# Retention heads: three rounded passes for most products, remainders on GpSimd, rings of two buffers, states updated in place

## The reference, cut to what matters

```
scores = einsum('bihd,bjhd->bhij', qc, kc) * decay_mask
intra  = einsum('bhij,bjhe->bihe', scores, vc)
cross  = einsum('bihd,bhde->bihe', qc * q_dec, S)
S_new  = S * chunk_dec + einsum('bjhd,bjhe->bhde', kc * k_dec, vc)
out    = intra + cross
```

## Time and profile before

| | us |
|---|---|
| median of 3 runs | 1812.44 (1810.49 to 1814.74) |
| the profiled execution | 1811.87 |
| its span | 1810.2 |
| TensorE busy in the span | 1758.1 |
| VectorE busy | 969.4 |
| ScalarE busy | 778.2 |
| GpSimd busy | 267.0 |

### The profile page before, as it was taken

One profiled execution on the slowest core, in us unless ns is written; L12 is line 12 of the kernel. 1 busy time (PEld: TensorE's weight loads), 2 busy tenths in 40 slices (PEclk: granted clock), 3 DMA queues, 4 the chain that ended last, 5 costly groups with the idle time before them and its releaser, 6 DMA issues. The chain is left out here.

```text
span 1810.2 us, 27358 instructions
## 1 busy us (share of the span) xinstructions
PE 1758.1 (97%) x9783; PEld 1388.7 (77%) x9783; DVE 969.4 (54%) x1867; ACT 778.2 (43%) x1683; POOL 267.0 (15%) x324
## 2 busy tenths in 40 slices
PE   5999999999999999999999999999998998999998
PEld 2678787878787878777788877788887777677677
DVE  4653535454444444453645554676625667777762
ACT  3742323232323232331434433353326768888720
POOL 2000000000000000000000011101113545555300
PEclk9999999999999999999999999999999999999999
DMA  9231312122222222366433578423365449696252
GB/s 338 87 97 60 95 61 89 67 79 76 75 80 68 87 61 93 104 209 217 130 84 116 190 231 271 157 80 112 102 186 134 123 117 251 194 236 190 86 192 93
DMA packets 153898, 240.60 MB, mean 133 GB/s; under 512 B 13289, under 2 KB 102177, under 8 KB 152770
## 3 DMA queue, kind: packets, MB, share of 16 engines
q1 hardware_dynamic: 136778, 179.69, 33.5%
q0 software_dynamic: 17024, 59.66, 9.3%
HBM read 177.91 MB, written 61.42 MB: 132 GB/s over the span
## 5 line engine op out<-in xcount | busy, mean ns | idle before, releaser
L488 PE MATMUL rt_acc<-rt_w_hi,rt_h_hi 128*128 128x512 f32 x504 | 203.3, 403 | 1.0 <-DVE rt_h_lo L1030 1.0
L490 PE MATMUL rt_acc<-rt_w_hi,rt_h_lo 128*128 128x512 f32 x504 | 197.1, 391 | 0.0
L489 PE MATMUL rt_acc<-rt_w_lo,rt_h_hi 128*128 128x512 f32 x504 | 196.5, 390 | 0.0
L1722 POOL TENSOR_TENSOR pa_take<-pa_take,pa_after_key 128x512 f32<-128x512 f32 (+2 forms) x152 | 153.3, 1011 | 141.7 <-DVE pa_after_key L2044 137.8
L1073 DVE TENSOR_TENSOR rt_by_cos<-rt_raw,rt_cos 128x256 f32<-128x256 f32 (+1 forms) x72 | 30.5, 424 | 243.9 <-ACT rt_raw L903 243.9
L914 ACT COPY rt_qk_t<-rt_tr 128x256 f32<-128x256 f32 (+1 forms) x72 | 26.0, 361 | 278.4 <-PE rt_tr L722 278.4
L2992 PE MATMUL kq_acc<-kq_w_hi,kq_h 128*128 128x512 f32 x320 | 128.6, 402 | 0.0
L2995 PE MATMUL kq_acc<-kq_w_hi,kq_h 128*128 128x512 f32 x320 | 125.1, 391 | 0.0
L2993 PE MATMUL kq_acc<-kq_w_lo,kq_h 128*128 128x512 f32 x320 | 124.7, 390 | 0.0
L1932 ACT ACTIVATE pa_keep<-z,pa_bias 128x128 f32<-128x128 f32 (+3 forms) x192 | 111.1, 600 | 5.9 <-PE z L1786 5.7
L1932 ACT ACTIVATE pa_take<-z,pa_bias 128x128 f32<-128x128 f32 (+3 forms) x192 | 111.1, 603 | 0.0
(11 more groups left out here) (406 smaller groups left out, 4025.8 us busy)
## 6 DMA issues: line engine op xcount, KB each, us to landing
ro_a_raw<-retained SPq DMA_DIRECT2D x14, 1024.0 KB, 6.0
rt_w_raw<-in_ret_w_in SPq DMA_DIRECT2D x16, 512.0 KB, 5.2
rt_w_raw<-in_ret_w_in SPq DMA_DIRECT2D x8, 1024.0 KB, 7.8
rt_old<-in_state_ret SPq DMA_DIRECT2D x8, 1024.0 KB, 5.9
rt_g_raw<-in_ret_w_in SPq DMA_DIRECT2D x8, 1024.0 KB, 5.2
out_st_sample<-rt_new POOLq DMA_DIRECT2D x8, 1024.0 KB, 7.9
k_cols<-kq_parts POOLq DMA_DIRECT2D x16, 512.0 KB, 4.0
kq_w_raw<-in_sb_w_in SPq DMA_DIRECT2D x4, 2048.0 KB, 10.2
```

The source lines that it names most:

```text
L488: nc.tensor.matmul(dst, h_hi[:, k, cols], w_hi[:, k, :], start=k == 0, stop=False)
L489: nc.tensor.matmul(dst, h_hi[:, k, cols], w_lo[:, k, :], start=False, stop=False)
L490: last = nc.tensor.matmul(dst, h_lo[:, k, cols], w_hi[:, k, :], start=False, stop=k == KD - 1)
L1722: nc.gpsimd.tensor_tensor(own, own, later, ALU.mult).then_inc(weighed, 1)
```

## The change

In heads 1 to 7, tiles 0 to 6, `attend` does its 20 products (two for tile 0, three for the others) in three rounded passes. The hi parts are made where the values are made: v_hi and q_hi by an added copy on ScalarE, k_hi, probs_hi and state_hi by an added instruction on VectorE. The remainders are made on GpSimd in a fixed order, and all count up one semaphore `rests`; `attend(t)` waits for the count `rests_by(h, t)` before its first matmul. v_lo lies over v and probs_lo over probs.

R becomes 2, and `probs` has one buffer. The samples' new states are written over `old`; `new` is gone. All stores move from GpSimd's queue to SyncE's, where the next `old` is loaded after the store of the one before. The waits `state_free`, `new_free` and `o_free` become waits for the stores themselves.

```diff
-        R = 3
+        R = 2
...
+        PARTED = NPT - 1
+
+        def parted(opens, t):
+
+            return not opens and t < PARTED
+
+        PER_HEAD = 5 * PARTED - 2
+
+        def rests_by(h, t):
+
+            kv, q, st, pr = 2 * min(t + 2, PARTED), min(t + 1, PARTED - 1), t, t + 1
+            return (h - 1) * PER_HEAD + (kv + q + st + pr)
...
+            def store_states(h):
+                sp.wait_ge(state_ready, after(h, NPT - 1))
+                sp.dma_start(t_out["st_prompt"][0, 0][bass.ds(h, 1)].rearrange("o k e -> (o k) e"), state[:]).then_inc(state_stored, 16)
+                sp.wait_ge(new_ready, h + (CR + 1))
+                sp.dma_start(t_out["st_sample"][0].rearrange("b h k e -> h k b e")[bass.ds(h, 1)].rearrange(
+                    "o k b e -> (o k) b e"), old[:]).then_inc(old_stored, 16)
+
+            def store_kept(h, cols):
+                kept = ps.retained[bass.ds(h * DV, DV), :].rearrange("(u p) c -> p u c", p=P)
+                sp.dma_start(kept[:, :, cols], o_t[:, :, cols]).then_inc(o_stored, 16)
+
+            load_old(0)
+            load_gates_of(0)
+            load_ada(0)
+            with sp.Fori(0, H - 1) as h:
+
+                sp.wait_ge(projected, h * NT + (NT + CR))
+                w_of.load(sp, t_in, h + 1)
+                store_states(h)
+                load_ada(h + 1)
+                sp.wait_ge(old_stored, h * 16 + 16)
+                load_old(h + 1)
+                load_gates_of(h + 1)
+                sp.wait_ge(o_out, h * TURNS + 4)
+                store_kept(h, slice(SEQ, SEQ + NS))
+                sp.wait_ge(o_out, h * TURNS + (TURNS + 1))
+                sp.sem_inc(storing, 1)
+                store_kept(h, slice(0, SEQ))
...
+            store_states(H - 1)
+            sp.wait_ge(o_stored, (H - 1) * 32)
...
+            def rest_of_state(h, t):
+                pool.wait_ge(state_ready, after(h, t))
+                nc.gpsimd.tensor_tensor(state_lo[:], state[:], state_hi[:].bitcast(F32), ALU.subtract).then_inc(rests, 1)
+
+            def rest_of_probs(h, t):
+                pool.wait_ge(masked, after(h, t))
+                nc.gpsimd.tensor_tensor(probs_lo[:], probs[:], probs_hi[:].bitcast(F32), ALU.subtract).then_inc(rests, 1)
+
+            def rest_of_q(h, t):
+                pool.wait_ge(turned_out, after(h, t))
+                nc.gpsimd.tensor_tensor(q_lo[:, t % R, :], qk_t[:, t % R, 0, :], q_hi[:, t % R, :].bitcast(F32),
+                                        ALU.subtract).then_inc(rests, 1)
+
+            def rest_of_v(h, t):
+                pool.wait_ge(taken, after(h, t))
+                nc.gpsimd.tensor_tensor(v_lo[:, t % R, :], v[:, t % R, :], v_hi[:, t % R, :].bitcast(F32), ALU.subtract).then_inc(rests, 1)
+
+            def rest_of_k(h, t):
+                pool.wait_ge(rotated, after(h, t))
+                nc.gpsimd.tensor_tensor(k_lo[:, t % R, :], rot[:, t % R, 1, :], k_hi[:, t % R, :].bitcast(F32),
+                                        ALU.subtract).then_inc(rests, 1)
+
+            with pool.Fori(1, H) as h:
+                for t in range(PARTED + 2):
+                    if 0 < t - 1 < PARTED:
+                        rest_of_q(h, t - 1)
+                    if 0 <= t - 3 < PARTED - 1:
+                        rest_of_state(h, t - 3)
+                    if 0 <= t - 2 < PARTED:
+                        rest_of_probs(h, t - 2)
+                    if t < PARTED:
+                        rest_of_v(h, t)
+                        rest_of_k(h, t)
...
+            def attend(h, t, opens):
+
+                r, slot, into = rows(t), t % R, out[0:rows(t), 0, 0:DV]
                 pe.wait_ge(o_taken, freed(h, t, 1))
                 if t == NPT:
+                    pe.wait_ge(masked, after(h, t))
                     pe.wait_ge(old_loaded, (h + 1) * 16)
                     pe.wait_ge(k_own_s, h + 1)
                     for i in range(2):
...
                             b, tokens = 4 * (c % 2) + 2 * (c // 2) + i, slice(32 * (c % 2), 32 * (c % 2) + 32)
                             nc.tensor.matmul(out[32 * c:32 * (c + 1), 0, 0:DV], q_diag[:, b, tokens], old[:, b, :], start=i == 0,
                                              stop=i == 1 and c >= 2, tile_position=(0, 32 * c))
-                elif t > 0:
-                    pe.wait_ge(state_ready, after(h, t - 1))
-                    nc.tensor.matmul(out[0:r, 0, 0:DV], qk_t[:, t % R, 0, :], state[:], start=True, stop=False)
-                last = nc.tensor.matmul(out[0:r, 0, 0:DV], probs[0:r, t % R, 0:r], v[0:r, t % R, :], start=t == 0, stop=True)
-                if t < NPT:
+                    nc.tensor.matmul(into, probs[0:r, 0:r], v[0:r, slot, :], start=False, stop=True)
+                elif parted(opens, t):
+                    pe.wait_ge(rests, rests_by(h, t))
+                    nc.tensor.matmul(into, probs_hi[:], v_hi[:, slot, :], start=True, stop=False)
+                    nc.tensor.matmul(into, probs_hi[:], v_lo[:, slot, :], start=False, stop=False)
+                    nc.tensor.matmul(into, probs_lo[:], v_hi[:, slot, :], start=False, stop=t == 0)
+                    if t:
+                        nc.tensor.matmul(into, q_hi[:, slot, :], state_hi[:], start=False, stop=False)
+                        nc.tensor.matmul(into, q_hi[:, slot, :], state_lo[:], start=False, stop=False)
+                        nc.tensor.matmul(into, q_lo[:, slot, :], state_hi[:], start=False, stop=True)
                     pe.wait_ge(state_ready, freed(h, t, 1) if t else h * NT + CR)
-                    last = nc.tensor.matmul(st[:, 0, 0:DV], rot[0:r, t % R, 1, :], v[0:r, t % R, :], start=True, stop=True)
+                    nc.tensor.matmul(st[:, 0, 0:DV], k_hi[:, slot, :], v_hi[:, slot, :], start=True, stop=False)
+                    nc.tensor.matmul(st[:, 0, 0:DV], k_hi[:, slot, :], v_lo[:, slot, :], start=False, stop=False)
+                    last = nc.tensor.matmul(st[:, 0, 0:DV], k_lo[:, slot, :], v_hi[:, slot, :], start=False, stop=True)
                 else:
+                    pe.wait_ge(masked, after(h, t))
+                    pe.wait_ge(state_ready, after(h, t - 1) if t else h * NT + CR)
+                    if t:
+                        nc.tensor.matmul(into, qk_t[:, slot, 0, :], state[:], start=True, stop=False)
+                    nc.tensor.matmul(into, probs[:], v[:, slot, :], start=t == 0, stop=True)
+                    last = nc.tensor.matmul(st[:, 0, 0:DV], rot[:, slot, 1, :], v[:, slot, :], start=True, stop=True)
+                if t == NPT:
...
+                if parted(opens, t):
+                    last.then_inc(raw_taken, 1)
+                    last = nc.scalar.copy(v_hi[:, t % R, :], src[:, 2 * DK:QKV])
                 last.then_inc(taken, 1)
...
-                nc.scalar.copy(qk_t[:, t % R, :, 0:r], src).then_inc(turned_out, 1)
+                last = nc.scalar.copy(qk_t[:, t % R, :, 0:r], src)
+                if t and parted(opens, t):
+                    last = nc.scalar.copy(q_hi[:, t % R, :], tr[:, 0, 0:P])
+                last.then_inc(turned_out, 1)
...
+                    dve.wait_ge(raw_taken, (h - 1) * PARTED + (t + 1))
...
+                    last = nc.vector.tensor_tensor(k_hi[:, t % R, :], by_cos[:, 1], by_sin[:, 1], ALU.add)
+                last.then_inc(rotated, 1)
...
+                dve.wait_ge(attended, freed(h, t, 1))
+                last = nc.vector.tensor_tensor(probs[0:r, 0:r], sc[0:r, 0, 0:r], table, ALU.mult)
+                if parted(opens, t):
+                    last = nc.vector.tensor_tensor(probs_hi[:], sc[:, 0, 0:P], table, ALU.mult)
+                last.then_inc(masked, 1)
...
-                    dve.wait_ge(state_free, h + 1)
+                    if not opens:
+                        dve.wait_ge(state_stored, h * 16)
+                    if parted(opens, t + 1):
+                        nc.vector.tensor_scalar(state_hi[:], st[:, 0, 0:DV], decay, None, ALU.mult)
                     nc.vector.tensor_scalar(state[:], st[:, 0, 0:DV], decay, None, ALU.mult).then_inc(state_ready, 1)
                 elif t < NPT:
                     dve.wait_ge(state_ready, after(h, t - 1))
                     nc.vector.tensor_tensor(state_sum[:], st[:, 0, 0:DV], state[:], ALU.add).then_inc(own, own_n.up())
                     dve.wait_ge(own, own_n.now())
+                    if parted(opens, t + 1):
+                        nc.vector.tensor_scalar(state_hi[:], state_sum[:], decay, None, ALU.mult)
                     nc.vector.tensor_scalar(state[:], state_sum[:], decay, None, ALU.mult).then_inc(state_ready, 1)
                 else:
                     join(h)
-                    dve.wait_ge(new_free, h + 1)
                     for n, src in enumerate((acc[:, 0], acc[:, 1], st[:, 0], tr[:, 0])):
                         pair = slice(2 * n, 2 * n + 2)
-                        last = nc.vector.tensor_tensor(new[:, pair, :], src.rearrange("p (b e) -> p b e", b=2),
```

(71 more changed lines are left out.)

51 lines of the change are left out of this document (21 added, 30 removed).

## The result

The changed kernel takes 1938.35 us (median of 4 runs, 1937.44 to 1939.40) against 1811.49 (4 runs, 1810.49 to 1814.74) for the kernel before in the same comparison. The ratio is 1.0695, 95% interval 1.0678 to 1.0712: 7% slower, 127 us. The forecast was 1905 with a range from 1868 to 1955, so the time is in the range and 33 us above its centre.

A forecast was written before the change was run, and what follows sets the result against it. TensorE, busy for 97% of the span, was taken to bound the kernel. Three passes -9.8, stalls +100.4, first head +1.5 and end +1 sum to +93 on 1811.87: 1905 us, range 1868 to 1955.

The forecast's parts named there:

- Gain of three passes: In seven heads, 20 products each take three rounded passes, 0.36 us in place of 0.43: 9.8 us gained.
- The queue order as the cause: attend(t) waits for probs_lo behind the next tile's q_lo on GpSimd: 14.3 us a head, 100.4 us lost in all.
- GpSimd's 128 columns: A remainder of 128 columns on GpSimd was priced at 0.41 us, from its rate on float32 products.
- the hand-over to TensorE: From a GpSimd result to TensorE's next start, 0.15 us was taken, between 0.05 and 0.3.
- attend(6), 0.76: At each head's attend(6), after the short sample tile, TensorE stalls 0.76 us because its own inputs come late.
- Head 0: In the first, float32 head, rings of two delay take and the input's splitting, before products 4 and 6: 1.5 us lost.
- The end: At the kernel's end the 1 MB state store stands ahead of two loads: 1 us lost, at worst 3.5.
- rival (c): TensorE's clock falls under repeated pauses, for half of each projection in 42 stalled tiles: 115 us more, 2020 us; chance 5%.
- both signs: Earlier clock readings: 0.67 with TensorE busy 6.41 of 10 us, but 1.00 with it busy 2.67 of 5.
- Rival (a): The remainders are hidden from TensorE, so the change gives its 9.8 us: 1802 us; chance 4%.
- (b): GpSimd is slow at the subtraction because writing the rounded type doubles its time: 1969 us, 1944 to 1980; chance 12%.
- (d): GpSimd's instructions overlap and short ones take less, so the middle five stalls are about 1 us: 1835 to 1870; chance 8%.

The follow-up runs named there:

- e2: The changed kernel with q's remainder moved behind those of state and probs in GpSimd's queue, and q counted one tile less in attend's wait: 1816.00 us.
- e5: e2 with rings of three for raw, rot, v and the hi and lo parts of k and v: 1805.42 us, ratio 0.9958 to the kernel before.
- e3: The changed kernel with a semaphore of its own for q's remainder, GpSimd's queue order left as it was: 1940.33 us.
- e7: The changed kernel with the remainder of probs computed twice on GpSimd, once into a tile nobody reads: 1967.01 us.
- e1: The changed kernel with eight unread 512-column matmuls on TensorE ahead of six of the seven waits in a head: 1914.96 us.
- e4: The changed kernel with all products in float32 and no GpSimd remainders, keeping rings of two, states in place and stores on SyncE: 1816.81 us.
- e6: The changed kernel with q's remainder between those of state and probs in GpSimd's queue: 1888.36 us.
- e8_g_later: e5 with VectorE's two remainders of the g weights moved behind rotate in their tiles: 1805.33 us.

## Why the prediction was right, and where its size was off

- **Gain of three passes, 9.8 us: right.** Steps of 0.12 after the first, and tiles of 7.00 in place of 7.21 wherever nothing waits (e2, e5).
- **The queue order as the cause, 100.4 us: right.** Forecast per head 1.73, five of 2.37 and 0.76; found 1.73 for attend(0), 2.41, and mostly 0.38 for attend(6), which makes 99 us. GpSimd's 128 columns took 0.45 and not 0.41, its 256 columns 0.72 and not 0.64, while the hand-over to TensorE was 0.06 (292.58 to 292.64) and not 0.15; these cancel. e2 shows the order as the cause, e3 clears the common semaphore, and e7 shows that each GpSimd instruction counts in full.
- **attend(6), 0.76: found 0.38 and, at the full clock in e1, 0.89.** The lower clock hides part of it.
- **Head 0, 1.5 us: right.** Before, TensorE waited once for h_lo in this head. It now waits three times, and the two new waits are 0.80 and 0.82 us, together 1.6, in TensorE's timeline:

```profile
79.61 0.50 PE L488 MATMUL rt_acc<-rt_w_hi,rt_h_hi 128*128 128x512 f32 x1 [0.80 <-DVE rt_h_lo L1106]
...
95.21 0.50 PE L488 MATMUL rt_acc<-rt_w_hi,rt_h_hi 128*128 128x512 f32 x1 [0.82 <-DVE rt_h_lo L1106]
```

- **The end, 1 us: found none.** ScalarE takes up the loaded block of the earlier trace rows at 904.36, 4 us before TensorE's product of that block, which starts at 908.37 with no wait, as before. The state store takes 4.4 us to land on SyncE's queue where it took 7.9 on GpSimd's. Row of the DMA issues:

```profile
out_st_sample<-rt_old SPq DMA_DIRECT2D x8, 1024.0 KB, 4.4
```

- **Left out: the first step after a pause.** It is 0.22 where the others are 0.12: 0.1 x 49 = 5 us.
- **The step that was off: the clock was left out of the sum.** I took it as rival (c) alone, at 115 us and 5%, priced as half of each projection in all 42 stalled tiles. In fact three tiles a head run at the lower level for some 3.4 us each (72 us in 21 tiles) and take 11.03 in place of 9.50. That is 1.53 x 21 = 32 us. In attend(6) it hides 0.5 x 7 = 3.5 of them, which the 99 above already leave out, so 28 to 29 remain to be gained; e1 gives 27 in the seven heads and 23 by the medians. So the mechanism of (c) was there at a quarter of its price, on top of the forecast and not in its place. The earlier trace rows held both signs, and I should have put a middle value into the sum instead of an all-or-nothing rival.

The account: -9.8 + 99 + 5 + 1.6 + 32 = 128 us, against 127 measured. e1's sum at the full clock is -9.8 + 103 + 5 + 1.6 = 100 us, and at the last head's sample tile its trace is 99.9 us behind the kernel before (853.73 against 753.88); the medians give 102.5. Less the clock and the first steps the measured 127 are 90, against a forecast of 93: the rest of the sum held, partly by errors that cancel. That the time lies in the stated range is in part luck: the range reached up to 1955 to allow for a slower GpSimd and slower hand-overs, and what filled it was mostly the clock.

Rival (a), remainders hidden, is what e2 and e5 make true: the 9.8 us came out as 6.7 in e5. Rivals (b) and (d) fall by the 0.45 and 0.72 us that the remainders took, one after the other without overlap.

What stays open: why the clock falls in every second tile and not in each, and why e4's median is 4 us above the kernel before when only some 2.5 are placed. For the first, e3 is a warning: its pauses and tiles are a little longer (2.33 in 9.57), and yet the lower level stands for less, 61 us in 18 stretches, and not in every second tile.

## What to carry to other kernels

When work moves to an idle engine, write down for each item when its input comes and when its output is due, and check the order of the queue against both. Here an item due a whole tile later stood ahead of the two that were due at once, which cost 122 of 127 us in a change that was to save TensorE time. Price repeated short pauses of TensorE twice, once as time and once as the chance of the lower clock behind them. And when a ring is shortened, look at the shortest tile, not the typical one: there the wait came first.

## What the runs showed of the hardware

- **The clock.** With pauses of 2.25 us in tiles of 9.50 it stood at 1.2 GHz for some 3.4 us in every second tile. With 1.57 in tiles of 8.82 it stayed at 2.4 GHz, with 2.66 the lower level came more often (120 us in all against 72, in e7's slowest execution), with 2.33 in tiles of 9.57 it came less often (61 us, e3), and with filler matmuls in the same 2.6 us it stayed at 2.4. Matmuls that nobody reads made this kernel 23 us faster. The Trainium skill (TensorE: Matmul & The Clock Gate, A second HAM failure mode: psum-queue depth-cycling) describes a kernel in which frequent short idle times between groups of matmuls make the clock swing between its two levels; the granted clocks of 0.50 and 1.00 in the windows above agree, and e6 shows that not every short pause does it.
- **GpSimd and VectorE hold each other up.** Side by side, probs_lo took 1.43 to 1.45 us in place of 0.45, g_lo 1.58 in place of 1.22, and v_lo 0.87 in place of 0.73, while VectorE's two by_sin products took 1.03 us together, against 0.49 in the kernel before, where GpSimd is idle. v_lo on GpSimd and these two, in the timeline of the changed kernel:

```profile
295.33 0.87 POOL L744 TENSOR_TENSOR rt_v_lo<-rt_v,rt_v_hi 128x256 fp32r<-128x256 f32 x1 [2.74 <-ACT rt_v_hi L977]
...
295.52 1.03 DVE L1154 TENSOR_TENSOR rt_by_sin<-rt_raw,rt_sin 128x128 f32<-128x128 f32 x2
```

  The Trainium skill (GPSIMD Engine Reference, 1 Specifications) states that GpSimd shares its SBUF interfaces with VectorE and contends with VectorE instructions that have two SBUF inputs; the rows agree. They look like one waiting for the other rather than both running slower. In e2_order probs_lo, begun during g_lo, ended 0.31 us after it (262.19 against 261.88), and g_lo was longer only where a GpSimd remainder was already running: 1.31 begun near the end of a k_lo, 1.58 begun early in a state_lo, and both of those kept their ordinary 0.46 and 0.73. In e8_g_later g_lo began first (163.05) and kept its 1.22, and k_lo, begun 0.16 us later, took 1.38 and ended 0.32 us after it. No run tests this by itself.
- **Writing the rounded type costs GpSimd little.** Its subtraction took 0.45 us for 128 columns and 0.72 for 256, against 0.41 (by rate) and 0.64 for the float32 product of the earlier trace rows.
